# Strict products of a delta rule scan, two batches ahead and among the blocks of the pull

## The reference, cut to what matters

```python
def rwkv_scan(inputs, S):
    def step(S, xs):
        r, v, kk, w, k, a = xs
        sa = jnp.einsum('bhvk,bhk->bhv', S, -kk)
        S = S * w[:, :, None, :] + sa[..., None] * (kk * a)[:, :, None, :] + v[..., None] * k[:, :, None, :]
        return S, jnp.einsum('bhvk,bhk->bhv', S, r)
    S, ys = lax.scan(step, S, tuple(jnp.moveaxis(t, 2, 0) for t in inputs))
    return jnp.moveaxis(ys, 0, 2), S
```

## Time and profile before

| what | value |
| --- | --- |
| median of 3 runs | 3025.61 us (3023.84 to 3027.55) |
| the profiled execution | 3031.57 us, its span 3029.8 us |
| PE busy | 2666.8 us (88% of the span) |
| DVE busy | 1277.9 us (42%) |
| ACT busy | 843.4 us (28%) |
| first scan, first strict product to last state update | 1016.3 to 1245.1 us |
| second scan, the same | 1248.6 to 1473 us |
| mean granted PE clock over the span | 0.924 |

### The profile page before, as it was taken

How to read it: one execution, slowest core, us unless ns; L and a number is a source line. 1 busy time by engine, 2 the same in 40 slices (tenths; PEclk the granted TensorE clock), 3 DMA queues, 4 the chain that set the end, 5 groups by cost and what they waited for, 6 DMA issues and landing times. The chain is left out here.

```text
span 3029.8 us, 47816 instructions
## 1 busy us (share of the span) xinstructions
PE 2666.8 (88%) x21060; PEld 1650.3 (54%) x21060; DVE 1277.9 (42%) x2007; ACT 843.4 (28%) x1522; POOL 117.9 (4%) x133
## 2 busy tenths in 40 slices
PE   7799999999899599899569779977977999989678
PEld 2454566666444488688434224433433867768533
DVE  3220434533576355355502232313513566656604
ACT  2111222233557255344220110101001334343301
POOL 0000000000112100000010000003000000000000
PEclk9799999999899799899879879987988999999779
DMA  6200111110556611110142530001012000010033
GB/s 242 78 28 6 57 41 47 56 47 18 146 156 147 162 59 32 64 59 32 71 188 97 213 120 28 28 13 49 28 56 90 22 22 15 1 42 1 14 153 97
DMA packets 89772, 214.00 MB, mean 71 GB/s; under 512 B 6245, under 2 KB 45285, under 8 KB 85978
## 3 DMA queue, kind: packets, MB, share of 16 engines
q1 hardware_dynamic: 79854, 173.58, 16.5%
q0 software_dynamic: 9712, 37.36, 4.8%
HBM read 155.87 MB, written 55.05 MB: 70 GB/s over the span
## 5 line engine op out<-in xcount | busy, mean ns | idle before, releaser
L689 PE MATMUL psum<-arena,m_fill_weight 128*128 128x512 f32 (+1 forms) x864 | 336.3, 530 | 5.8 <-DMA m_fill_weight<-in_l_w_in 5.8
L2353 PE MATMUL psum<-arena,g_weight 128*128 128x512 f32 (+1 forms) x512 | 219.0, 554 | 27.6 <-DMA g_weight<-in_l_w_in 27.6
L389 PE MATMUL psum<-arena,project_weight_y 128*128 128x512 f32 x512 | 221.7, 596 | 13.1 <-DMA project_weight_y<-in_l_w_in 13.1
L689 PEld LDWEIGHTS psum<-arena,m_fill_weight 128*128 128x128 f32 x864 | 157.8, 194 | 108.3 <-issue 91.8
L389 PEld LDWEIGHTS psum<-arena,project_weight_y 128*128 128x128 f32 x512 | 97.8, 191 | 137.7 <-issue 123.0
L389 PE MATMUL psum<-arena,project_weight_m 128*128 128x512 f32 (+3 forms) x432 | 158.2, 530 | 15.0 <-DMA project_weight_m<-in_l_w_in 15.0
L2599 DVE COPY_PREDICATED g_pairs<-g_masks,psum 128x512 f32<-128x512 uint8 x128 | 93.5, 730 | 142.5 <-PE psum L2381 142.5
L1166 PE MATMUL psum<-gp_weight,arena 128*128 128x512 f32 x320 | 149.9, 617 | 0.0
L2344 PE MATMUL psum<-g_weight,arena 128*128 128x128 f32 x1152 | 145.0, 275 | 0.0
L2103 PE MATMUL psum<-out_weight,arena 128*128 128x512 f32 x256 | 113.8, 607 | 29.1 <-DMA out_weight<-in_l_w_out 29.1
L2112 PE MATMUL psum<-out_weight,arena 128*128 128x512 f32 x320 | 137.7, 592 | 0.0
(11 more groups left out here) (381 smaller groups left out, 4192.3 us busy)
## 6 DMA issues: line engine op xcount, KB each, us to landing
mod_weight<-in_l_mod_w SPq DMA_DIRECT2D x16, 1536.0 KB, 7.5
arena<-scratch_operands SPq DMA_DIRECT2D x40, 512.0 KB, 4.0
scratch_operands<-arena POOLq DMA_DIRECT2D x16, 640.0 KB, 8.2
scratch_operands<-arena POOLq DMA_DIRECT2D x32, 320.0 KB, 11.2
g_weight<-in_l_w_in SPq DMA_DIRECT2D x20, 512.0 KB, 4.6
m_fill_weight<-in_l_w_in SPq DMA_DIRECT2D x18, 512.0 KB, 3.8
out_weight<-in_l_w_out SPq DMA_DIRECT2D x16, 512.0 KB, 10.9
project_weight_y<-in_l_w_in SPq DMA_DIRECT2D x4, 2048.0 KB, 8.0
```

The lines of the kernel that those rows point to most:

```text
L389: last = nc.tensor.matmul(p.psum[0:rows, u % 8, 0:n], lhsT, rhs, start=(k == 0), stop=(k == KT - 1))
L689: last = nc.tensor.matmul(p.psum[:, FILL + f % BANKS, 0:width], weight[:, q % PIECES, k, :], hT[:, k, at:at + width], start=(k == 0), stop ...
L2353: last = nc.tensor.matmul(bank[:, 0:width], w[:, kk, :], hT[:, kk, first:first + width], start=(kk == 0), stop=(kk == KT - 1))
```

## The change

The strict products of both lanes of a batch are now one block with one increment of `strict_ready`. Those of batch b+2 are made inside `pull(b)`: after the two products of the pull for a pair j come the two strict products of the same lane and pair. Those of batches 0 and 1 are made at the start of the scan, batch 0 ahead of `products(0, 0)` and batch 1 behind `products(0, 1)`, both ahead of the first `turn_inverse`. The two places behind the half products are left out. DVE waits for the same number in both lanes.

```diff
--- before.py
+++ after.py
@@ -1566,14 +1566,20 @@
 
             @block.tensor
             def _(pe):
-                def strict_products(b, lane):
+                def strict_product(b, lane, j, q):
                     s = 2 * b + lane
-                    pe.wait_ge(operands_loaded[s % SLOTS], 16 * (s // SLOTS + 1))
-                    if s:
-                        pe.wait_ge(strict_read, s)
-                    for j, q in both:
-                        last = nc.tensor.matmul(bank(STRICT)[part(q), at(lane, j)], queries(s)[part(q), j, q, :],
-                                                keys(s)[part(q), j, q, :], start=True, stop=True)
+                    return nc.tensor.matmul(bank(STRICT)[part(q), at(lane, j)], queries(s)[part(q), j, q, :],
+                                            keys(s)[part(q), j, q, :], start=True, stop=True)
+
+                def strict_products(b):
+                    for lane in range(2):
+                        s = 2 * b + lane
+                        pe.wait_ge(operands_loaded[s % SLOTS], 16 * (s // SLOTS + 1))
+                    if b:
+                        pe.wait_ge(strict_read, 2 * b)
+                    for lane in range(2):
+                        for j, q in both:
+                            last = strict_product(b, lane, j, q)
                     last.then_inc(strict_ready, 1)
 
                 def products(b, lane):
@@ -1615,13 +1621,26 @@
                     last.then_inc(v_turned, 1)
 
                 def pull(b):
+
+
                     pe.wait_ge(v_copied, 2 * (b + 1))
                     pe.wait_ge(state_ready, 2 * b + 1)
+                    if b + 2 < B:
+                        for lane in range(2):
+                            s = 2 * (b + 2) + lane
+                            pe.wait_ge(operands_loaded[s % SLOTS], 16 * (s // SLOTS + 1))
+                        pe.wait_ge(strict_read, 2 * (b + 2))
                     for lane in range(2):
-                        for j, q in both:
-                            last = nc.tensor.matmul(bank(CHAIN)[part(q), at(lane, j)], prod[part(1 - q), b % 2, lane, q, j, part(q)],
-                                                    uv[part(1 - q), b % 2, lane, q, j, :], start=True, stop=True)
+                        for j in range(J):
+                            for q in range(2):
+                                last = nc.tensor.matmul(bank(CHAIN)[part(q), at(lane, j)], prod[part(1 - q), b % 2, lane, q, j, part(q)],
+                                                        uv[part(1 - q), b % 2, lane, q, j, :], start=True, stop=True)
+                            if b + 2 < B:
+                                for q in range(2):
+                                    strict = strict_product(b + 2, lane, j, q)
                     last.then_inc(pulled_ready, 1)
+                    if b + 2 < B:
+                        strict.then_inc(strict_ready, 1)
 
                 def begin_chunk(b, lane):
                     s = 2 * b + lane
@@ -1694,16 +1713,15 @@
                                                     half[part(r), q, four(lane, jj), :], start=True, stop=True)
                     last.then_inc(upper_ready, 1)
 
+                strict_products(0)
                 for lane in range(2):
-                    strict_products(0, lane)
                     products(0, lane)
+                strict_products(1)
                 turn_inverse(0, 1)
                 for b in range(B):
                     half_product(b, 1)
                     if b:
                         begin_chunk(b - 1, 0)
-                    if b + 1 < B:
-                        strict_products(b + 1, 0)
                     upper_product(b, 1)
                     if b:
                         solve_chunk(b - 1, 0)
@@ -1721,8 +1739,6 @@
                     half_product(b, 3)
                     if b:
                         begin_chunk(b - 1, 1)
-                    if b + 1 < B:
-                        strict_products(b + 1, 1)
                     upper_product(b, 3)
                     if b:
                         solve_chunk(b - 1, 1)
@@ -1841,7 +1857,7 @@
 
                 def read_strict(b, lane):
                     s = 2 * b + lane
-                    dve.wait_ge(strict_ready, s + 1)
+                    dve.wait_ge(strict_ready, b + 1)
                     if b >= 2:
                         dve.wait_ge(half_ready, TOP * (b - 1))
                     nc.vector.tensor_tensor(strict_t[:, b % 2, lane], narrow(bank(STRICT)[:, lane * HALF:(lane + 1) * HALF]),
```

## The result

| | before | after |
| --- | --- | --- |
| median, 22 runs each | 3024.73 us | 3036.82 us |
| profiled execution (span) | 3031.57 us (3029.8) | 3044.31 us (3042.5) |
| mean granted PE clock | 0.924 | 0.925 |

After over before is 1.0037, with a 95% interval of 1.0027 to 1.0047: slower by 8 to 14 us. The medians differ by 12.1 us, the profiled executions by 12.7 us. Times in the two traces are shifted against each other by what lies ahead of the scan, so I count from the issue of a scan's first operand load: 1012.41 and 1245.36 us before, 1008.99 and 1247.57 after.

The account below looks back on a forecast made before the run. The tensor engine looked fully busy, but ScalarE's copy of the half product was taken to set the path, strict blocks being cover. 0.5 + 3.5 + 1.8 = 5.8 us took the median from 3025.61 to 3031.4 us, range 3023 to 3042.

Parts of the forecast that it names:

- Removed from the gaps, worth nothing: Half product to upper product: 2 x 0.46 us of strict work per batch, beside ScalarE's copy, gains nothing when removed.
- Alternation in the pull, 0.5 us: Pull, batches 0 to 7 of both scans: 0.03 us each for later starts and added waits, bounds 0 and 14.7.
- a scan's batches each as long as before: Steady batches of both scans: a sign of the forecast, wrong if one gets shorter by more than 0.1 us.
- The bound above (14.7): Pull, both scans: upper bound if strict and pull passes do not overlap, 16 x 0.92 us.
- Rival 2: Pull: alternation does not overlap, 14.7 us instead of 0.5, giving 3045.6 us; chance 0.11.
- First scan's start, 3.5 us: First scan's start: upper product 5.4 us late, less 1.85 for a quicker passage; bounds 2.6 to 5.4.
- Second scan's start, 1.8 us: Second scan's start: strict products wait for chunk 1, turn at 1259.9 instead of 1258.13; bounds 0.9 and 3.7.
- its upper bound of 3.7: Second scan's start: loss if the clock comes up one passage later, 1.85 us more.
- Sum: Whole kernel: alternation and both scan starts add 5.8 us, median 3031.4 us.
- Rival 3: Starts of both scans: clock comes up sooner, loss only 1.7 to 3.5 us, 3027.3 to 3029.1; chance 0.20.

Follow-up runs that it names:

- strict_few: Kernel before, with only the first of each lane's 8 strict products made from batch 1 on: 3020.62 us against 3023.43, ratio 0.9997.
- start_only2: Changed start of both scans, batches as in the kernel before: 3028.83 us against 3025.23, ratio 1.0023.
- after_pad: Changed kernel plus 32 one-column products (128 records) at each scan's start: 3038.90 us against 3025.23 for the kernel before, ratio 1.0054.
- after_pad16: Changed kernel plus 16 one-column products (64 tensor instructions) at each scan's start, one run: 3040.93 us.
- before with the same pad: Kernel before plus one-column products at each scan's start: with 32, 3026.11 us against 3025.23, ratio 1.0005; with 16, 3029.98 us.
- block_behind_pull: Start as before; strict products of batch b+2 as one block of 16 products behind the pull: 3037.25 us against 3023.43 before, ratio 1.0048.
- early_operands: Kernel before, scan 1's chunk 2 and 3 loads ahead of the values, first values turn behind level 2's upper product: 3024.43 us against 3026.59, ratio 0.9990.

## Why the prediction was right, and where not

**Removed from the gaps, worth nothing: right in a steady batch.** 1.49 us in after and with 2 passes in strict_few.

**Alternation in the pull, 0.5 us: the mechanism right, the cost wrong.** The block itself is free, and a clean batch is 20.29 us. But "a scan's batches each as long as before" failed, and this is the term that was mis-sized: 5.2 us in the profiled pair, 4.6 by the means over all positions (2 x 2.3), not 0.5. The bound above (14.7) was made for a lack of overlap, and that was the wrong reason for a high cost. I counted quadrants and did not ask whether instructions come fast enough for 128 of them in 1.03 us. The trace before held the hint: waits by "issue" in mid block, 0.4 to 0.5 us each, in scan 2.

**Rival 2 (no overlap): refuted.** Pull and strict products together are 64 passes in 1.03 us, not 1.95. That alone would leave room for the pull's passes in turn at 32 ns each, the strict ones beside them in the other bank. The rows decide against it: the two passes of the one product in strict_few, alone in their quadrant, start 0.06 us apart (0.28 us for the two, 0.22 for one), and 32 such passes one behind the other would be 1.9 us. The pull takes 1.03, so its two row halves write one bank side by side. The Trainium skill, TensorEngine Tiling (Array Packing), Gotcha 1: PSUM Pressure, has that different row tiles cannot access one bank simultaneously; this trace does not agree.

**First scan's start, 3.5 us: 2.7, within its bounds 2.6 to 5.4.** The first upper product came 5.5 us late (predicted 5.4); two misses cancel in that, as the strict products began 1.7 us later by the first load (1.27 predicted) and half to upper product took 1.67 us instead of 1.93. From there to the first pull 2.8 us came back instead of 1.85, since the clock was up behind the half product already.

**Second scan's start, 1.8 us: 3.8, just above its upper bound of 3.7.** The turn came 14.0 us after the second load's issue at 1247.97 (predicted 14.2), 1.65 us later by the first load's. The other 2.1 us are the clock: it rose one passage later, as the bound had it. The gap from half to upper product, which the strict products no longer fill, went ahead of that. The runs support this gap as the cause. From the second scan's first upper product to its first pull, the seven kernels with the gap filled take 15.5 to 16.5 us, and three of the five with it unfilled 18.2 to 18.8: after, start_only2, and strict_few, where the list differs from before's by the gap alone (its clock, though, had already been up once ahead of it). The other two, after_pad and after_pad16, take 15.5; their clock had risen just before the first turn.

So how much a start costs hangs on where the clock stands, and one pair of traces is partly luck. The change of the start lost 2.7, 3.7, 5.9 and 3.5 us in the first scan and 3.8, 2.9, 1.0 and 1.2 in the second (after, start_only2, and the two padded kernels against before with the same pad), on average 4.0 and 2.2 against 3.5 and 1.8 predicted.

**Sum.** 0.5 + 3.5 + 1.8 = 5.8 predicted; 5.2 + 2.7 + 3.8 = 11.7 found. The direction held and the median, 3036.8 us against 3031.4 forecast, lies in the range. That is partly luck: nearly half of the loss comes from a term that I had put near nothing, for a reason that I had not considered. **Rival 3** (clock up sooner in both scans) held in the first scan and failed in the second. Open: why a packet starts soon after the border before in one place and 2 us later in another, which decides whether the next piece comes in time.

## What to carry to other kernels

Work that stands in the gap of a wait is free, and moving it into a dense block can cost even where the array has room; at a stage's start, where the clock is low, the filled gap can be worth something. Look for idle time by "issue" inside a block, number the engine's instructions, and see whether the stops share a place modulo 256. Shifting the stream by dummy instructions moved most of these stops but did not remove them; with the same products in the gaps there were fewer. At a stage's start, work that waits for a late load belongs behind the first steps of the chain that do not need it.

## What the runs showed of the hardware

- TensorE's instruction stream arrives in packets of 16384 bytes, one for 256 records (167 packets, 42745 records). No border between two pieces was passed sooner than 2.17 us after its packet's start (964 borders in twelve traces). Where PE is faster it stops: all 43 stops of over 0.5 us between passes of one block stand at record 194 or 195 modulo 256, and in before and after they end 2.3 to 2.9 us after such a packet's start.
- 64x64 passes on the two diagonal quadrants and on the other two run side by side if they alternate: 64 passes in 1.03 us as 32 alone. As one block behind the other they cost 0.76 us more (block_behind_pull).
- Two row halves write one PSUM bank side by side: 32 passes in 1.03 us, where two passes in one quadrant start 0.06 us apart.
- In early_operands the granted clock fell from 1.00 to 0.50 behind an idle time of 2.81 us and rose again at 1039.1 us, behind tensor work.
